# A hybrid decoder step: products with sides exchanged, queries never turned, decode memory attention by quarters of the array, and start-up loads moved between queues

## The chip, the cores and the metric

The kernel runs on one core of a Trainium2 chip. The time is the device time of that core in microseconds, the median of the runs shown. All arithmetic is in 32-bit floats. TensorE takes every 32-bit matmul as two instructions, so the trace shows two records for each matmul of the source; a transposition is one record.

## The reference, cut to what matters

One layer works on 1024 prompt tokens and 32 decode tokens (8 sequences of 4).

```
P = RMSNorm(x) @ w_in              # one projection, cut into the parts of three groups
A: mLSTM    4 heads x 256, in chunks of tokens, with a state matrix C and vector n per head
B: sparse   4 heads x 128, rotary; an indexer picks 256 keys per query; softmax; * silu(z)
C: memory   s = q . mem_k ; a = softmax(s) ; o = a . mem_v ; * silu(z)   (4 heads x 128, 256 memory rows)
y = x + RMSNorm(concat(A, B, C) @ w_out)
```

In group C the prompt attends to one set of memory keys, and each decode sequence b to its own (`cache_mem_k[b]`, `cache_mem_v[b]`, 256 x 512 each).

In group A, per head and chunk of 128 tokens, with decays:

```
s   = (q k^T) * decay ;   num = s v + inter * (q C)
C   = decay * C + (w k)^T v
```

## The kernel before, in words

Four stages run one after another: `project_rotate`, `select`, `attend_bc` and `mix_out`. Between two stages all engines meet (the wait is recorded at line 113) and the semaphores are cleared. Inside a stage each engine has its own list of instructions, written out in order, and waits on semaphores; DMAs are issued from SP's list, a few from ACT's and POOL's. Nothing reorders a list.

**project_rotate.** x is normalised, turned and kept as `xT` (model dimension on the partitions, tokens along the free axis). Most columns of w_in are multiplied in "tiles" (128 tokens by one block of columns, line 1065). Six blocks of 512 columns (`QUADS`) are multiplied by the seven-product scheme (`quad`, line 1129): the 2 x 2 blocks of x and w are summed by DVE, seven products of 512 tokens x 1024 x 256 columns are made, and ACT and DVE combine them out of PSUM. A product is four groups t = 0..3 of 128 tokens; each has 8 matmuls in which x is the stationary side and 256 columns of w move. Group t writes `bank[t][:, 0:256]`. Results are stored as rows of the scratch tensor `proj` (token by column). The decode tokens are done beside them by `quad_decode`.

Three of the six blocks are the memory queries (`C_MQ`) and the mLSTM queries (`C_Q`, `C_Q + 512`). While the later tiles are multiplied, rows of `proj` come back (`load_r`, line 713): queries and keys of group B, index queries and the memory queries. DVE and POOL rotate those of group B (`rotary`, lines 795 to 801); then PE turns five groups g per tile of 128 tokens (`turn_group`, line 1032; g = 0 is the memory queries), ACT copies each out of `rbank` (`keep_group`, line 942) and stores them in `headT`, the scratch tensor of turned heads. `hooks` says after which matmul of which tile each group is turned. The rotation of tile n + 1 waits until the stores of tile n have landed.

**select** picks the keys; it also projects the columns that are left. Near its end `ahead` loads the prompt memory keys, the decode memory keys of sequences 0 and 1, and the decode memory values of sequences 0 to 4 into the half of `w` that is free.

**attend_bc** first finishes what concerns the decode tokens, then walks through 32 units (8 tiles of 128 tokens x 4 heads) plus a lag of 6 slots, after which its share of w_out is multiplied (line 1933). The part for the decode tokens comes in this order on PE: turn the prompt memory keys (1836); wait for `lk_ready`, that is for DVE, which waits for twelve small DMAs (`small_in`); turn the selected logits (1842) and probabilities (1850); then for each of the 32 pairs of a sequence and a head turn its memory keys (two transpositions, 1869), ACT copies them (2040), DVE clears a 128 x 128 slot `pz` and puts the four queries in their columns (2152, 2153), and one matmul of 128 rows x 256 memory rows adds into `bank[4]` (1882); softmax over all rows at once (2159 to 2165); then 16 matmuls with a cleared slot each against 512 columns of memory values (1895), of which every row is kept for its own head only (`own_head`). SP loads the other six key tiles in a loop as their buffers come free (1767). DVE's `dec_clear` lets the 32 units begin.

**mix_out** does the mLSTM of group A and the rest of w_out. It walks through slots s = -2 .. 36: unit s + 2 is turned (`turn`, 2820: two transpositions for q, two for k), unit s + 1 gets its products of q and k (2831), unit s its numerator (2843, 2845) and its new state (2856); from s = 5 on (LAG) the output of an earlier chunk is multiplied by w_out (2882) in the same slot, and from s = 1 on one decode sequence and head per slot is done (2894, 2902). Unit n = 4 c + h is chunk c and head h. SP loads a unit with six DMAs (`load`, 2353 to 2355), unit s + 4 at the end of slot s. At its start SP issues, in this order: the gate rows, unit 0, seven tables (2366 to 2374), unit 1, `dv`, eight decode states (2379), units 2 and 3, two blocks of w_out of 2 MB (2385), the first rows of the partial output (2359), `g_post` (2387), and in slot 0 another 25 small DMAs (2394 to 2402), then the second partial rows.

## Time and profile before

| | |
|---|---|
| median of 3 runs | 3103.03 us (3101.26 to 3108.2) |
| the profiled execution, its own time | 3105.0 us |
| its span, first to last instruction | 3103.3 us |
| PE busy | 2944.9 us, 95% |
| DVE, ACT, POOL busy | 1399.9, 451.0, 404.1 us |
| mean granted clock of TensorE | 0.973 of full speed |
| project_rotate | 0 to about 1098 us |
| select | about 1098 to 2182 us |
| attend_bc | about 2182 to 2648 us |
| mix_out | about 2648 to 3103 us |

The page gives busy times of each engine over the span. A matmul's record includes its way through the array, so the time that a matmul costs in a long row of them is the distance between two starts: the length of a group less one record, divided by the number of records less one. A granted clock of 1.00 is 2.4 GHz, and 0.50 is 1.2 GHz. An idle time in square brackets stands ahead of the instruction, with what ended it.

### The profile page before, as it was taken

How to read it: one execution, taken by the hardware profiler on the slowest of the kernel's cores; microseconds unless marked ns; L12 is line 12 of the kernel's file. 1: busy time of each engine (PE TensorE's matmuls, PEld its weight loads, DVE VectorE, ACT ScalarE, POOL GpSimd, SP SyncE). 2: the span in 40 equal slices, each digit the busy share in tenths (PEclk: the TensorE clock that was granted, in tenths of full speed). 3: DMA queues.
4: the chain of work that ended last, by engine and by line, in shares of the span. 5: the costliest groups of instructions: out<-in, count | busy, mean ns of one | idle time of the engine just before them, and what ended most of it. 6: DMA issues, size and time to landing. Idle time of an engine off the chain costs nothing. (4 is left out here: it accounts for less than half of the span.)

```text
span 3103.3 us, 36094 instructions
## 1 busy us (share of the span) xinstructions
PE 2944.9 (95%) x13209; PEld 1757.9 (57%) x13209; DVE 1399.9 (45%) x2480; ACT 451.0 (15%) x970; POOL 404.1 (13%) x567
## 2 busy tenths in 40 slices
PE   8999999999999979999999999999689999499998
PEld 6678888888644434444444444444455564355553
DVE  3241111111121226899999998554332231244553
ACT  3210000000011135100000300000232221122221
POOL 0000000000022200000000000264013100233432
PEclk9999999999999988999999999999899999699999
DMA  6512112221526351320210521376464212745642
GB/s 235 119 33 77 61 46 68 75 70 50 170 83 199 113 194 27 116 73 20 75 72 20 182 73 55 108 240 197 139 207 150 90 49 85 245 128 182 193 148 90
DMA packets 248895, 353.59 MB, mean 114 GB/s; under 512 B 42412, under 2 KB 164756, under 8 KB 243484
## 3 DMA queue, kind: packets, MB, share of 16 engines
q1 hardware_dynamic: 207436, 269.86, 26.9%
q0 software_dynamic: 14784, 61.88, 6.4%
q10 hardware_dynamic: 26544, 20.08, 2.2%
q8 instruction: 87, 1.43, 0.2%
q14 instruction: 44, 0.36, 0.0%
HBM read 267.86 MB, written 86.43 MB: 114 GB/s over the span
## 5 line engine op out<-in xcount | busy, mean ns | idle before, releaser
L276 PE MATMUL sbank<-w,xT 128*128 128x512 f32 x2048 | 882.6, 593 | 6.6 <-ACTq L227 2.9
L276 PEld LDWEIGHTS sbank<-w,xT 128*128 128x128 f32 x2048 | 389.1, 190 | 496.2 <-issue 489.3
L1065 PE MATMUL bank<-w,xT 128*128 128x512 f32 (+1 forms) x768 | 290.9, 534 | 0.0
L1129 PE MATMUL bank<-w,xT 128*128 128x256 f32 x1152 | 253.9, 380 | 0.0
L1129 PEld LDWEIGHTS bank<-w,xT 128*128 128x128 f32 x1152 | 217.8, 190 | 30.3
L1933 PE MATMUL at_bank_bc<-w,at_hT 128*128 128x512 f32 x512 | 230.0, 593 | 3.9 <-ACT at_bc_out L2091 3.9
L1129 PE MATMUL bank<-w,area 128*128 128x256 f32 x960 | 212.1, 379 | 0.0
L1065 PEld LDWEIGHTS bank<-w,xT 128*128 128x128 f32 x768 | 143.4, 191 | 121.3 <-issue 106.2
L897 DVE TENSOR_TENSOR pout<-pout,bank 128x256 f32<-128x256 f32 x120 | 50.5, 421 | 339.6 <-PE bank L1129 339.6
L1129 PEld LDWEIGHTS bank<-w,area 128*128 128x128 f32 x960 | 182.4, 190 | 24.8
L1579 DVE MATCH_REPLACE8 area<-m,area 128x384 f32<-128x384 f32 (+2 forms) x192 | 165.7, 876 | 0.0
L1576 DVE MAX8 m<-area 128x8 f32<-128x384 f32 (+2 forms) x192 | 155.5, 879 | 11.9 <-DVE area L1579 11.9
L1933 PEld LDWEIGHTS at_bank_bc<-w,at_hT 128*128 128x128 f32 x512 | 94.6, 190 | 103.0 <-issue 101.6
L250 ACT ACTIVATE pout_b<-sbank 128x512 f32<-128x512 f32 x64 | 37.9, 598 | 787.8 <-PE sbank L276 787.8
L795 POOL TENSOR_TENSOR area<-area 128x288 f32<-128x288 f32 (+1 forms) x9 | 11.7, 1299 | 907.3 <-DMA area<-in_rot 727.3
L853 DVE TENSOR_TENSOR w<-w 128x2048 f32<-128x2048 f32 x24 | 54.4, 2288 | 166.6 <-PE bank L1129 163.2
L1129 PE MATMUL bank<-w 128*128 128x256 f32 x576 | 129.2, 379 | 0.0
L1129 PEld LDWEIGHTS bank<-w 128*128 128x128 f32 x576 | 109.4, 190 | 14.9
L2882 PE MATMUL mo_bank_acc<-mo_w_out_a,mo_hT 128*128 128x512 f32 x256 | 116.2, 598 | 0.0
L2882 PE MATMUL mo_bank_acc<-area,mo_hT 128*128 128x512 f32 x256 | 116.2, 598 | 0.0
L795 DVE TENSOR_TENSOR area<-area 128x512 f32<-128x512 f32 (+1 forms) x9 | 6.2, 691 | 201.8 <-DMA headT<-area 184.9
L980 ACT ACTIVATE pout<-bank 128x256 f32<-128x256 f32 x48 | 18.4, 384 | 502.0 <-PE bank L1129 502.0
(384 smaller groups left out, 3324.7 us busy)
## 6 DMA issues: line engine op xcount, KB each, us to landing
w<-in_w_in SPq DMA_DIRECT2D x18, 2048.0 KB, 12.5
w<-in_w_in SPq DMA_DIRECT2D x28, 1024.0 KB, 5.3
area<-in_x_prompt SPq DMA_DIRECT2D x16, 1024.0 KB, 7.4
proj<-pout_b SPq DMA_DIRECT2D x64, 256.0 KB, 2.1
proj<-pout SPq DMA_DIRECT2D x96, 128.0 KB, 1.7
headT<-area ACTq DMA_DIRECT2D x8, 1024.0 KB, 9.2
area<-roped_q_of_decode POOLq DMA_DIRECT2D x32, 256.0 KB, 3.9
w<-in_w_out SPq DMA_DIRECT2D x4, 2048.0 KB, 15.9
```

Source lines behind the costliest of these rows:

```text
L250: copy(pout[:, j, 0:self.w], bank[:, 0:self.w], function).then_inc(self.copied, 1)
L276: last = k.nc.tensor.matmul(bank[0:r, 0:self.w], k.xT[:, c, r0:r0 + r], k.w[:, u, c, 0:self.w], start=c == 0, stop=c == KT - 1)
L795: order(ops.tensor_tensor(o1, x1, cos, ALU.mult))
L853: nc.vector.tensor_tensor(quarter[out], quarter[x], quarter[y], op).then_inc(w_sums, 1)
L897: nc.vector.tensor_tensor(out[:, t, :], x[:, t, :], bank[t][:, 0:256], ALU.add).then_inc(sums_read, 1)
L980: nc.scalar.activation(out[:, t, :], bank[t][:, 0:256], ACT.Copy).then_inc(first_read, 1)
L1065: last = nc.tensor.matmul(dst[:, 0:wd], k.xT[:, c, t * P:(t + 1) * P], wc, start=c == 0, stop=c == KT - 1)
L1129: last = nc.tensor.matmul(bank[t][:, 0:256], x(c, t), at[name][:, c, :], start=first and c == 0, stop=c == 7, skip_group_check=True)
L1576: order(nc.vector.max(m8[:, j, :], x))
L1579: order(nc.vector.match_replace(out=x, in_to_replace=m8[:, j, :], in_values=x, imm_value=TAKEN))
L1933: last = nc.tensor.matmul(acc[:, :], hT[:, t % 2, j, :], w[:, j, b * O_W:(b + 1) * O_W], start=j == 0, stop=j == HT - 1)
L2882: last = nc.tensor.matmul(acc[n % 2][:, :], hT[:, c % 2, j, :], w[b][:, j, :], start=j == 0, stop=j == HT - 1)
```

## The change

1. **Sides exchanged in three of the six seven-product blocks** (`TURNED`: memory queries and both halves of the mLSTM queries). In them the weights are the stationary side, 128 columns at a time, and 512 tokens move: two groups (t = 1 and t = 3) of 8 matmuls of 512 in place of four groups of 8 matmuls of 256. A group fills a whole bank, `bank[0]` or `bank[2]`, and counts as two; ACT and DVE read the same 128 x 256 pieces as before through `product_at`. The results come out turned, and are stored so: the memory queries into `headT`, the mLSTM queries into a new scratch tensor `qT`.
2. **No turning of queries later.** In `project_rotate` the memory queries of the eight prompt tiles are neither loaded, nor turned, copied or stored again (the decode tile still is). ACT's store of a tile into `headT` is two DMAs that leave the four memory-query slots out. In `mix_out` a unit's q is loaded turned (from `qT`, 256 rows of 128 tokens), `turn` has two transpositions in place of four, ACT's copy is 256 wide in place of 512, and `dots` and `scaled_q` read the loaded q.
3. **Decode memory attention by quarters.** `ahead` loads five key tiles and two value tiles; the other three and six are loaded at the start of `attend_bc`. All decode queries are spread once into `dmq_of`. Per sequence PE turns all four heads (8 transpositions into two banks), ACT and DVE copy one bank each, and four matmuls, each into its own 32 rows of `bank[4]`, add the dots. This comes before the work on the selected logits, whose instructions DVE does between the copies. The values are 64 matmuls of 32 rows x 128 columns out of a spread tile, each for its own head, so that `own_head` goes for this part.
4. **Loads at the start of `mix_out`.** SP issues only the gate rows and units 0 to 3. ACT issues the tables and `dv` (8 DMAs) ahead of its first copy, four decode states in slot -1 and four in slot 1. POOL issues the two blocks of w_out in slot 0 and `g_post` in slot 2. The partial rows come in slot 1 on SP, the 25 small DMAs in slot 10 (`LATE`), and DVE's two instructions that need them in slot 14.

The core of the diff:

```diff
+    TURNED = [C_MQ, C_Q, C_Q + 512]
...
+        def product_at(n, t):
+            return bank[t // 2 * 2][:, 256 * (t % 2):256 * (t % 2) + 256] if fp.QUADS[n] in fp.TURNED else bank[t][:, 0:256]
...
+        def group(n, g):
+            return 4 * n + g - 1 if n < QT else 4 * QT + g
+        def stored_all(n):
+            return 80 * n
...
             if q >= 2 and q % 2 == 0:
-                found.update({0: (q // 2 - 1, 4), 12: (q // 2, 0)})
+                found[0] = (q // 2 - 1, 4)
...
-            if q == 1:
-                found[1] = (0, 0)
+            if q == 2 * QT:
+                found[12] = (QT, 0)
...
-                act.dma_start(k.headT[:, 0:T_IK, at_], keep_at[:, 0:T_IK, 0:r]).then_inc(r_stored, 16)
+                if n < QT:
+                    for a, b in ((T_Q, T_MQ), (T_IQ, T_IK)):
+                        act.dma_start(k.headT[:, a:b, at_], keep_at[:, a:b, 0:r]).then_inc(r_stored, 16)
+                else:
+                    act.dma_start(k.headT[:, 0:T_IK, at_], keep_at[:, 0:T_IK, 0:r]).then_inc(r_stored, 16)
...
                         for c in range(8):
-                            last = nc.tensor.matmul(bank[t][:, 0:256], x(c, t), at[name][:, c, :],
-                                                    start=first and c == 0, stop=c == 7, skip_group_check=True)
-                        last.then_inc(product, 1)
+                            if whole:
+                                u = t // 2
+                                last = nc.tensor.matmul(bank[2 * u][:, :], at[name][:, c, P * u:P * (u + 1)], x(c, 0, SEQ // 2),
+                                                        start=first and c == 0, stop=c == 7, skip_group_check=True)
...
+                        last.then_inc(product, 2 if whole else 1)
...
+            def turn_mkd(b):
+                if b < 5:
+                    pe.wait_ge(mkd_in[b], 16)
+                else:
+                    pe.wait_ge(mkd_late[b - 5], 16)
+                if b >= 2:
+                    pe.wait_ge(mkd_kept_a, b - 1)
+                    pe.wait_ge(mkd_kept_v, b - 1)
+                for h in range(H):
+                    for c in range(2):
+                        last = nc.tensor.transpose(
+                            bank[(5, 2)[b % 2] + h // 2][:, N_MEM * (h % 2) + P * c:N_MEM * (h % 2) + P * (c + 1)],
+                            mkd[b % 5][:, c, h * DH:(h + 1) * DH], k.ident[:])
+                last.then_inc(mkd_turned, 1)
+            def dots_mkd(b):
+                pe.wait_ge(mkd_kept_a, b + 1)
+                pe.wait_ge(mkd_kept_v, b + 1)
+                for h in range(H):
+                    last = nc.tensor.matmul(bank[4][NS * h:NS * (h + 1), 0:N_MEM], dmq_of[:, h, NS * b:NS * (b + 1)],
+                                            mkdT[:, b % 2, h, :], start=b == 0, stop=b == DEC_B - 1)
+                last.then_inc(mdots, 1)
...
+            for b in range(DEC_B):
+                for c in range(2):
+                    for h in range(H):
+                        last = nc.tensor.matmul(bank[6][NS * h:NS * (h + 1), 0:DH], spread[:, c, h, NS * b:NS * (b + 1)],
+                                                mvd[:, 2 * b + c, h * DH:(h + 1) * DH], start=b + c == 0,
+                                                stop=b == DEC_B - 1 and c == 1)
...
+    LATE = 10
...
-                for dst, c0 in ((q, C_Q), (kk, C_K), (o, C_O), (z, C_Z)):
+                sp.dma_start(q[:, r, :, :], k.qT[h * ML_D:(h + 1) * ML_D, at].rearrange("(c p) t -> p c t", p=P)
+                             ).then_inc(loaded[r], 16)
+                for dst, c0 in ((kk, C_K), (o, C_O), (z, C_Z)):
...
+            def load_states(b):
+                for h in range(ML_H):
+                    act.dma_start(ds[:, ML_H * b + h, :, 0:ML_D], ins["state_mlstm_C"][b, h].rearrange("(c p) v -> p c v", p=P)
+                                  ).then_inc(d_state_in[ML_H * b + h], 16)
...
+                if s == 0:
+                    for b in range(2, O_B):
+                        nc.gpsimd.dma_start(w[b], ins["w_out"][0:ML_W, b * O_W:(b + 1) * O_W]
+                                            .rearrange("(c p) n -> p c n", p=P)).then_inc(w_in[b], 16)
+                if s == 2:
+                    nc.gpsimd.dma_start(g[:], ins["g_post"][0:1, :].partition_broadcast(P)).then_inc(g_in, 16)
...
-                for x, at in ((q, 0), (kk, 2)):
-                    for c in range(2):
-                        last = nc.tensor.transpose(tq[:, (at + c) * P:(at + c + 1) * P],
-                                                   x[:, n % 4, c * P:(c + 1) * P], k.ident[:])
+                for c in range(2):
+                    last = nc.tensor.transpose(tq[:, c * P:(c + 1) * P], kk[:, n % 4, c * P:(c + 1) * P], k.ident[:])
```

## Rows read from the trace of the kernel before

**Rows 1.** Windows: length, then busy us of PE, PEld, DVE, ACT, POOL, clock, DMA, GB/s.
```profile
2150.00:2250.00 100.00, 73.96 (x368) 43.84 (x366) 26.46 (x121) 17.33 (x43) 7.57 (x8) 0.86 0.46 153
...
2660.00:2710.00 50.00, 22.45 (x111) 16.53 (x112) 12.47 (x45) 6.79 (x19) 15.32 (x28) 0.64 0.97 309
...
2680.00:2685.00 5.00, 4.63 (x34) 3.32 (x35) 1.89 (x6) 0.50 (x2) 1.65 (x3) 1.00 1.05 394
...
2720.00:2730.00 10.00, 7.93 (x25) 5.76 (x25) 5.06 (x20) 1.94 (x5) 3.14 (x6) 0.67 0.51 132
...
2900.00:3000.00 100.00, 100.00 (x378) 58.41 (x377) 48.50 (x139) 20.95 (x58) 36.16 (x59) 1.00 0.54 169
```
**Rows 2.** Waits of PE: waiter, releaser, us in total, times, longest.
```profile
PE mo_bank_turn_qk L2820 <- DMA mo_rows_everywhere<-gate_rows: 31.5, 4, 16.8
```
**Rows 3.** Timeline of PE, projection: start, us, line, tiles, count, [idle before].
```profile
111.82 20.77 PE L1057 MATMUL bank<-w,memT 128*128 128x512 f32 x48
...
259.61 13.98 PE L1129 MATMUL bank<-w,xT 128*128 128x256 f32 x64
```
**Rows 4.** Timeline of PE while heads are turned in the projection.
```profile
826.67 1.11 PE L1032 MATMUL rbank<-ident_sb,area 128*128 128x128 f32 x4 [2.84 <-DMA area<-in_rot]
...
833.64 0.60 PE L1032 MATMUL rbank<-ident_sb,area 128*128 128x128 f32 x4
834.08 2.74 PE L1065 MATMUL bank<-w,xT 128*128 128x512 f32 x6
...
956.06 0.66 PE L1032 MATMUL rbank<-ident_sb,area 128*128 128x128 f32 x4 [1.87 <-DVEq L904]
```
**Rows 5.** The page, part 6: a DMA, count, KB each, us to landing.
```profile
headT<-area ACTq DMA_DIRECT2D x8, 1024.0 KB, 9.2
```
**Rows 6.** Timeline of PE from the last projection to the first unit of attend_bc.
```profile
2171.35 3.70 PE L273 MATMUL sbank<-w,xT 128*32 128x128 f32 x128
2181.66 1.94 PE L1836 MATMUL at_bank_dots<-ident_sb,w 128*128 128x128 f32 x8 [6.61 <-PEq L113]
2193.95 0.69 PE L1842 MATMUL at_bank_mem<-ident_sb,at_lk 128*128 128x128 f32 x2 [10.35 <-DVEq L2133]
...
2235.12 14.00 PE L1895 MATMUL at_bank_bc<-w,at_pz 128*128 128x512 f32 x32
...
2251.75 0.49 PE L1919 MATMUL at_bank_dots<-area,at_qT 128*128 128x128 f32 x2 [1.77 <-DVEq L2184]
```
**Rows 7.** Timeline of DVE and DMA issues, start of attend_bc.
```profile
2182.35 1.98 DVE L2116 MEMSET at_p_spread<- 128x2304 f32 x1 [0.43 <-issue]
...
at_dec_mqT<-headT SPq DMA_DIRECT2D x1, 64.0 KB, 3.2
```
**Rows 8.** Timeline of PE, start of mix_out.
```profile
2653.71 0.69 PE L2820 MATMUL mo_bank_turn_qk<-ident_sb,mo_q 128*128 128x128 f32 x2 [3.03 <-DMA mo_rows_everywhere<-gate_rows]
...
2678.02 0.44 PE L2820 MATMUL mo_bank_turn_qk<-ident_sb,mo_q 128*128 128x128 f32 x2
...
2702.54 0.69 PE L2820 MATMUL mo_bank_turn_qk<-ident_sb,mo_q 128*128 128x128 f32 x2 [16.84 <-DMA mo_rows_everywhere<-gate_rows]
...
2710.74 0.38 PE L2820 MATMUL mo_bank_turn_qk<-ident_sb,mo_q 128*128 128x128 f32 x2
...
2731.45 3.60 PE L2882 MATMUL mo_bank_acc<-area,mo_hT 128*128 128x512 f32 x8
```
**Rows 9.** Timeline of SP's DMA issues, start of mix_out.
```profile
2650.41 0.57 SPq L2355 DMA_DIRECT2D mo_rows_everywhere<-gate_rows  x1
...
2694.35 0.43 SPq L2355 DMA_DIRECT2D mo_rows_everywhere<-gate_rows  x1
```
**Rows 10.** Timeline of PE, one steady slot of mix_out.
```profile
2766.20 0.38 PE L2820 MATMUL mo_bank_turn_qk<-ident_sb,mo_q 128*128 128x128 f32 x2
2766.42 0.38 PE L2820 MATMUL mo_bank_turn_qk<-ident_sb,mo_k 128*128 128x128 f32 x2
...
2777.59 0.38 PE L2820 MATMUL mo_bank_turn_qk<-ident_sb,mo_q 128*128 128x128 f32 x2
```

More of the change, by code:

```diff
@@ L1019, in turn_group @@
                 if g == 0:
-                    pe.wait_ge(r_loaded[u], 80 * (n // 2 + 1))
-                    heads = [mq[0:r, u, h * DH:(h + 1) * DH] for h in range(H)]
+                    pe.wait_ge(mq_in, 16)
+                    heads = [mq[0:r, h * DH:(h + 1) * DH] for h in range(H)]
                 elif g < 3:
@@ L1090, in quad @@
                         (of(rows_d), "22", False))):
-                    for t in range(4):
+                    whole = fp.QUADS[n] in fp.TURNED
+                    for t in (1, 3) if whole else range(4):
+                        opening = t == 1 if whole else t == 0
                         if phase == 0:
-                            if t == 0:
+                            if opening:
                                 loaded("11")
@@ L1128, in quad @@
                         for c in range(8):
-                            last = nc.tensor.matmul(bank[t][:, 0:256], x(c, t), at[name][:, c, :],
-                                                    start=first and c == 0, stop=c == 7, skip_group_check=True)
-                        last.then_inc(product, 1)
+                            if whole:
+                                u = t // 2
+                                last = nc.tensor.matmul(bank[2 * u][:, :], at[name][:, c, P * u:P * (u + 1)], x(c, 0, SEQ // 2),
+                                                        start=first and c == 0, stop=c == 7, skip_group_check=True)
+                            else:
+                                last = nc.tensor.matmul(bank[t][:, 0:256], x(c, t * P, (t + 1) * P), at[name][:, c, :],
+                                                        start=first and c == 0, stop=c == 7, skip_group_check=True)
+                        last.then_inc(product, 2 if whole else 1)
             at = None
@@ L2113, in _, with keep_mkd @@
             order = Order(dve, order_sem)
-            for ap, value in ((ones, 1.0), (zero, 0.0)):
-                order(nc.vector.memset(ap[:], value))
+            nc.vector.memset(dmq_of[:], 0.0).then_inc(dmq_set, 1)
+            order(nc.vector.memset(ones[:], 1.0))
+            dve.wait_ge(dmq_in, 16)
+            dve.wait_ge(dmq_set, 1)
+            nc.vector.tensor_copy(dmq_of[:, :, :].rearrange("p h (b x) -> p h b x", x=36)[:, :, :, 0:DEC_T],
+                                  dmq[:, :, :].rearrange("p h (b t) -> p h b t", t=DEC_T)).then_inc(dmq_set, 1)
+            def keep_mkd(b):
+                dve.wait_ge(mkd_turned, b + 1)
+                if b >= 2:
+                    dve.wait_ge(mdots, b - 1)
+                nc.vector.tensor_copy(mkdT[:, b % 2, 2:4, :].rearrange("p a b -> p (a b)"), bank[(5, 2)[b % 2] + 1][:, :]
+                                      ).then_inc(mkd_kept_v, 1)
+            for b in range(4):
+                keep_mkd(b)
             nc.vector.memset(spread[:], 0.0).then_inc(masks, 1)
-            dve.wait_ge(small_in, 16 * (4 + 2 * DEC_T))
+            keep_mkd(4)
+            keep_mkd(5)
+            dve.wait_ge(small_in, 16 * (3 + DEC_T))
             for c in range(2):
```

323 lines of the change are left out of this document (153 added, 170 removed).

## The prediction, written before the change was run

> **What bounds the kernel now.** I read the windows by stretch first. In a steady stretch late in the kernel PE is busy all the time at full clock: there only work taken off PE counts [rows 1]. Two stretches are different. Where attend_bc begins, PE is idle 26 us of 100, and where mix_out begins, it is busy only 22.45 us of 50, with DMA at 97% [rows 1]. Next the waits of PE: the longest sum is 31.5 us in four waits, all for a unit of mix_out that had not been loaded [rows 2]. Then the timeline of PE, for the order within these two starts [rows 6, 8], and that of the projection, for what a transposition or a product costs [rows 3, 4]. So the terms to look for are PE work removed where PE is full, and idle time removed at the two starts.
>
> **Part 1, the exchanged products.** A record of 256 moving columns costs (13.98 - 0.379) / 63 = 0.2159 us, taking the 0.379 us of one record off; one of 512 columns costs (20.77 - 0.597) / 47 = 0.4292 us [rows 3]. A block of seven products has 7 x 4 x 8 x 2 = 448 records now, 96.7 us, and 224 after, 96.1 us: 0.6 us each, 1.8 us for three. The reads of ACT and DVE keep their number and size. A group now lasts 16 x 0.43 = 6.9 us and the next one that writes the same bank begins 6.9 us after it ends, while its two reads take under 1 us, so no wait is added. Bounds: 0 (if the new form costs what two of the old do) and 3 us. I take 1.8.
>
> **Part 2a, the memory queries no longer turned in the projection.** Four transpositions hold PE from 833.64 to 834.08, 0.44 us [rows 4]. Eight tiles make 3.5 us. For tile 0 they save nothing: the rotation that the next group needs starts when `load_r` has landed (the wait that ended at 826.67 [rows 4]) and takes some 7 us, so the 2.84 us wait moves from the first group to the second. It ends earlier only by the 256 KB less that come before, 0.8 us. So 0.8 + 7 x 0.44 = 3.9 us. The single wait of 1.87 us at 956.06, for the rotation of tile 4 [rows 4], hangs on the store of `headT`, 1 MB in 9.2 us [rows 5]. A quarter of those bytes goes, some 2 us, so I take this wait as gone too: 5.8 us in all. The extra DMA issue per tile is on ACT, mostly idle here. Bounds: 2 us (store no faster, tile 0 nothing, half of the transpositions hidden) and 7.
>
> **Part 3, decode memory attention.** Before, from 2181.66 to 2251.75, 70.1 us [rows 6]. It holds a 10.35 us wait for small DMAs and 14.00 us of value matmuls [rows 6]. After:
> - 2181.66 to 2183.4: prompt memory keys turned, as before. The clock is at 1.2 GHz here: 8 transpositions cost (1.94 - 0.42) / 7 = 0.217 us each [rows 6]. The first sequence is turned until 2185.1.
> - The decode queries are now SP's first DMA of the stage. It took 3.2 us to land [rows 7], so it is there at 2184.9. Clearing `dmq_of` (1152 columns) is half of the 1.98 us that 2304 took [rows 7], and is done by then. PE goes on at 2185.3.
> - Eight sequences. At half clock one costs 8 x 0.217 = 1.74 us of transpositions, and 8 records of dots. Four matmuls into four quarters ran side by side in the projection: 128 records of 128 columns in 3.70 us, 0.029 us each at full clock [rows 6]; at 256 columns and half clock that is 0.11, so 0.9 us. Together 2.6 us, at full clock 1.3. The copies (0.6 us on ACT, 0.7 on DVE, my estimate from other 128x512 reads) fit beside. DVE's extra 2 us memset and the logits add about 2 us at full clock. Half of the sequences at each clock: 4 x 2.6 + 3 x 1.4 + 2 = 17 us, to 2202; all at half clock, to 2206.
> - The tail: softmax of the memory rows, two turnings, softmax of the selected rows, then 128 records at 0.029, 3.7 us, one copy. With some ten short steps of 0.2 to 0.7 us between: 10.5 us at full clock, 14 at half.
> The first unit then starts between 2212 and 2220, instead of 2251.75: 32 to 39 us, and I take 35. What could hold it is data: before the values can be used, three key tiles, six value tiles (4.5 MB) and 2 MB of gathered values must land in the 24 us from 2182. That needs 270 GB/s, and DMA has moved 394 in a busy stretch [rows 1]. Outer bounds 22 and 43. The six value tiles, the prompt values and units 0 and 1 are queued behind SP's waits for key buffers, but those end by 2190. The w_out loads keep their distance to the values' end.
>
> **Part 4, the start of mix_out.** Now: the first unit is turned at 2653.71, the fourth at 2678.02 (slot 1), the fifth only at 2702.54 after 16.84 us idle, and the first w_out product starts at 2731.45 in slot 5 [rows 8]. The fifth unit's last DMA was issued at 2694.35, 44 us after the first unit's [rows 9], since 25 small DMAs and 8 MB of others stood ahead in SP's list.
> - After, units 0 to 3 are issued one behind the other, 3 us each. The constants come 3 to 4 us sooner, from ACT. POOL's and DVE's work of slots -1 and 0 is unchanged and becomes the chain. I put slot 1 at 2670, 8 us sooner (bounds 4 and 12).
> - Unit 4 is issued when slot 0 ends and should land within slot 1, so the 16.84 us go. Slots 1 to 4 each take what slots 3 and 4 take now: (2731.45 - 2710.74) / 2 = 10.3 us at a mean granted clock of 0.67 [rows 1, 8], or about 7.7 at full clock, as slot 1 did. With 9.5: slot 5 at 2670 + 38 = 2708, 23 us sooner. Bounds: all at 10.3 with slot 1 at 2674, 2715; all at 7.7 from 2666, 2697: 16 to 34 us. A late unit takes more off (rival 1).
> - POOL issues 4 MB with two instructions; I take 1 us each, behind its wait for DMAs.
>
> **Part 2b, steady slots of mix_out.** PE is full there, and the two q transpositions hold it from 2766.20 to 2766.42, 0.22 us of an 11.39 us slot [rows 10]. Slots 5 to 29: 25 x 0.22 = 5.5 us. The new q load moves the same bytes in pieces half as long. The 25 small DMAs in slot 10 take SP some 12 us, one slot. Unit 14 is then issued about 5 us late, with some 5 us to spare: I charge 0.5 us (0 to 3). Net 5.0.
>
> **Sum.** 1.8 + 5.8 + 35 + 23 + 5.0 = 70.6 us. The profiled execution took 3105.0 us (span 3103.3), 2 us more than the median 3103.03; its differences carry over to the median: 3032 us. Its own range, with the bounds not all on one side, is 3017 to 3046.
>
> **Rival 1: bytes, not issue order, hold mix_out's start.** Before unit 5 can be turned (slot 3, 2687 by my working), the queues hold units 0 to 5 (4.7 MB), tables 0.9, states 2.1, w_out 4.2, partial rows 2.1, x 1.05 and g 1: 16 MB. At the 309 GB/s of the stretch 2660 to 2710 [rows 1] this takes 52 us from 2648, to 2700: 13 us late. For it: DMA is already at 97% there, and SP issues 3 MB of partial rows and x ahead of unit 5. Against it: 394 GB/s was reached at 2680 [rows 1], by which it is 2689, and w_out, on another queue, need not be through. Part 4 then gives 10 instead of 23: 3045 us. The Trainium skill ("DMA: Bandwidth & Descriptors", section "Issuing engines are not separate DMA queues") states that DMAs issued by SP, ACT and POOL interleave on the same 16 engines, so that issuing from several saves only the sequencer's time. By that rule alone moving w_out to POOL buys no room, which is this rival; the DMA share of 97% in rows 1 agrees with it.
>
> **Rival 2: the decode part stays a chain.** If TensorE stays at half clock and the late tiles or DVE's list hold each sequence to 4 us (32 us for eight, and a 14 us tail), the first unit starts at 2232: part 3 gives 20 instead of 35, 3047 us. For it: after the present idle time the clock stayed at 0.50 for long. Against it: PE has far fewer gaps.
>
> **Rival 3: slower.** The half-long pieces of q make a unit's loads land late in every steady slot. Unit s + 4 is issued in 2.7 us at the end of slot s and is wanted one slot, 11.2 us, later: it decides when landing takes over 8.5 us, and PE then loses what is over. At 11.5 us it loses 3 us in each of 27 slots, 81 us against the 76 that the rest gives: 3108 us. For it: stores in such pieces took 9.2 us, but for 1 MB [rows 5]; a unit's q is 128 KB. Against it: the steady DMA share is 0.54 [rows 1].
>
> That the change does not do what it says: if the turned blocks cost two reads' wait per group, 42 groups x 0.8 us = 34 us come back, 3066 us. The waits are a whole group away, so I give it little.
>
> **Chances.** Forecast 0.58, rival 1 0.23, rival 2 0.12, rival 3 0.02, the last 0.03, else 0.02. Faster or slower by 0.2% is 6 us, about what a measurement of this kernel can tell: faster 0.95, same 0.02, slower 0.03. The range takes in the rivals 1 and 2 and the bounds of parts 3 and 4: 3013 to 3055.
>
> **What would show it.** Right: records of 128x512 in the three blocks at 0.429 us apart; no wait at L1032's first group but one on the rotation; the first unit of attend_bc some 31 to 39 us after the stage's first transposition instead of 70; turns of unit 4 without a long wait, and 43 to 61 us, some 54, from the first turn of mix_out to its first w_out product, instead of 78; steady slots of 11.2 us. Wrong: PE waiting on DMAs for units 4 to 6, or on the value tiles; a slot at s = 12 with a wait; reads in the blocks that PE waits for.

## The result and the profile after

The changed kernel takes 3055.57 us (median of 4 runs, 3044.59 to 3060.49) against 3105.61 for the kernel before in the same comparison (3101.26 to 3109.45): ratio 0.9838, interval 0.9821 to 0.9854, 50 us less. The forecast was 3032 us, 70.6 us less than the 3103.03 known then: the time is 24 us above it and half a microsecond above the end of its range, 3055, and 20 us of the gain are missing. Three executions far from all others (6806.11 us in experiment 1, 3534.25 and 12586.81 us of the kernel before, taken beside experiments 9 to 12) are left out of every median and ratio here. The profiled execution is the slowest of the four, 3060.49 us with a span of 3058.8; its gain is 44.5 us. The four executions are 3060.49, 3059.81, 3051.32 and 3044.59 us, twice as far apart as those of before; that turns out to be part of the answer.

The first part of the page: PE has 28.5 us less to do, in 12529 matmuls, and its share of the span is 95% as before.

```profile
PE 2916.4 (95%) x12529; PEld 1607.7 (53%) x12529; DVE 1387.1 (45%) x2392; ACT 429.8 (14%) x937; POOL 405.2 (13%) x570
```

The waits of PE in the changed kernel (in all, times, longest). Before, the first line had 31.5 us with one wait of 16.8 [rows 2]; the line with L276 was not there at all.

```profile
PE mo_bank_turn_qk L2886 <- DMA mo_rows_everywhere<-gate_rows: 17.3, 4, 7.3
...
PE sbank L276 <- issue: 10.2, 2, 5.6
...
PE rbank L1062 <- DVEq L930: 4.4, 1, 4.4
PE mo_bank_dots_num L2908 <- DVE mo_sd L2513: 4.3, 1, 4.3
PE at_bank_turn L1906 <- DVE w L2169: 4.3, 3, 2.4
```

**Projection.** The timeline of PE where the seven-product blocks end and the tiles begin (start, duration, line, count, and in brackets the idle time before and what ended it):

```profile
794.43 10.03 PE L1164 MATMUL bank<-w 128*128 128x512 f32 x23
804.30 19.90 PE L1095 MATMUL bank<-w,xT 128*128 128x512 f32 x46
828.60 1.12 PE L1062 MATMUL rbank<-ident_sb,area 128*128 128x128 f32 x4 [4.40 <-DVEq L930]
829.51 3.93 PE L1095 MATMUL bank<-w,xT 128*128 128x512 f32 x6
...
1089.37 2.89 PE L1401 MATMUL sbank<-ident_sb,w 128*128 128x128 f32 x12 [9.97 <-PEq L113]
```

The 23 records of the exchanged products take (804.30 - 794.43) / 23 = 0.429 us each, as forecast. The first group turned is now a rotated one and waits 4.40 us for DVE, where 2.84 and 1.87 us were idle before [rows 4]. Select's first transposition starts at 1089.4 instead of 1098.3.

**Select**, which the change doesn't touch, gives all of that back and more: attend_bc's first transposition starts at 2187.50, 5.8 us *later* than before [rows 6]. The windows (length, busy time of PE, PEld, DVE, ACT and POOL, granted clock, DMA share, GB/s) and the timeline of PE at the two idle stretches:

```profile
1700.00:1710.00 10.00, 9.02 (x141) 5.52 (x139) 9.68 (x18) 0.88 (x2) 0.00 (x0) 1.00 0.07 26
1710.00:1720.00 10.00, 5.34 (x7) 2.37 (x8) 9.47 (x19) 2.54 (x3) 0.00 (x0) 0.66 0.75 219
```

```profile
1714.66 20.60 PE L276 MATMUL sbank<-w,xT 128*128 128x512 f32 x42 [5.64 <-issue]
...
1949.42 8.96 PE L276 MATMUL sbank<-w,xT 128*128 128x512 f32 x14 [4.60 <-issue]
```

PE idles 5.64 and 4.60 us waiting for nothing that a semaphore shows ("issue"). Both stand where TensorE jumps back to the head of its loop over the select stage's column blocks (line 282). The loop has four iterations of some 230 us, each of two blocks of 114, and so three jumps back: the first, near 1480 us, passes without idle time, the second and the third don't. Behind it the clock falls to its lower level, 1.2 GHz: 0.66 on the mean of 1710 to 1720. The stage's block products take 936.7 us instead of 922.0, 7.3 us for each of the two, of which 5.1 are idle. The DMA view of the same stretch says what moved. Changed kernel, 1600 to 2100 us:

```profile
DMA packets 27368, 59.26 MB, mean 119 GB/s; under 512 B 3111, under 2 KB 3623, under 8 KB 27352
## 3 DMA queue, kind: packets, MB, share of 16 engines
q8 instruction: 16, 0.26, 0.2%
```

Sixteen packets of 16 KB of instructions; the same view of the kernel before has no row for q8. There the last packet of instructions comes at 1487 us, in the first iteration, and the next at 2209, behind the stage: three jumps back with nothing read. Its loop runs from what it has at hand, and the changed kernel's is read again.

**Decode memory attention**, timeline of PE: first transposition, a wait for copies, the value products, the first attend unit.

```profile
2187.50 1.94 PE L1881 MATMUL at_bank_dots<-ident_sb,w 128*128 128x128 f32 x8 [6.63 <-PEq L113]
...
2197.49 1.08 PE L1906 MATMUL at_bank_turn<-w,at_dec_mqT_spread 128*32 128x256 f32 x8 [2.39 <-DVE w L2169]
...
2215.46 6.43 PE L1941 MATMUL at_bank_bc<-w,at_p_spread 128*32 128x128 f32 x128 [2.28 <-DMA w<-in_cache_mem_v]
...
2222.45 0.49 PE L1966 MATMUL at_bank_dots<-area,at_qT 128*128 128x128 f32 x2 [0.55 <-DVEq L2226]
```

From the first transposition to the first unit it is 34.95 us instead of 70.1 [rows 6].

**Start of mix_out**, timeline of PE: the stage's first product, the turning of units 0, 3, 4, 5 and 6, and the first product with w_out (slot 5).

```profile
2620.80 1.05 PE L2975 MATMUL mo_bank_acc<-ident_sb,mo_y 12*128 12x12 f32 x9 [9.03 <-DMA mo_y<-gate_rows]
2629.13 0.69 PE L2886 MATMUL mo_bank_turn_qk<-ident_sb,mo_k 128*128 128x128 f32 x2 [7.28 <-DMA mo_rows_everywhere<-gate_rows]
...
2645.53 0.44 PE L2886 MATMUL mo_bank_turn_qk<-ident_sb,mo_k 128*128 128x128 f32 x2
...
2660.66 0.44 PE L2886 MATMUL mo_bank_turn_qk<-ident_sb,mo_k 128*128 128x128 f32 x2 [4.57 <-DMA mo_rows_everywhere<-gate_rows]
...
2671.50 0.56 PE L2886 MATMUL mo_bank_turn_qk<-ident_sb,mo_k 128*128 128x128 f32 x2 [3.03 <-DMA mo_rows_everywhere<-gate_rows]
...
2679.12 0.38 PE L2886 MATMUL mo_bank_turn_qk<-ident_sb,mo_k 128*128 128x128 f32 x2
...
2689.51 1.02 PE L2947 MATMUL mo_bank_acc<-area,mo_hT 128*128 128x512 f32 x2
```

From first turn to first w_out product 60.4 us instead of 77.7 [rows 8]. But the first turn itself is 8.3 us behind the stage's first product; it was 4.1. From 2645 to 2671 us, where units 4 and 5 are late, the DMA engines are busy throughout (share 1.04, 387 GB/s).

**Steady slots**, timeline of PE, and the first and the last of the 25 small transfers of slot 10 on SyncE's queue. The slots are 11.17 us apart (before 11.39 [rows 10]); behind slot 10 unit 14 is late once.

```profile
2701.48 0.38 PE L2886 MATMUL mo_bank_turn_qk<-ident_sb,mo_k 128*128 128x128 f32 x2
2712.65 0.38 PE L2886 MATMUL mo_bank_turn_qk<-ident_sb,mo_k 128*128 128x128 f32 x2
...
2772.14 0.44 PE L2886 MATMUL mo_bank_turn_qk<-ident_sb,mo_k 128*128 128x128 f32 x2 [2.44 <-DMA mo_rows_everywhere<-gate_rows]
```

```profile
2750.84 0.47 SPq L2431 DMA_DIRECT2D mo_dec_o<-proj  x1
...
2762.35 0.43 SPq L2439 DMA_DIRECT2D mo_dec_y<-y_of_groups_b_c_decode  x1
```

### The profile page after: what moved, and what is told of

Read it like the earlier page. It is cut to its first block and busy times, and to the rows that moved or that the text cites. A ratio compares the mean times of both kernels' runs of the same rounds, so it can differ in the third digit from the quotient of the medians.

```text
span 3058.8 us, 34334 instructions
## 1 busy us (share of the span) xinstructions
PE 2916.4 (95%) x12529; PEld 1607.7 (53%) x12529; DVE 1387.1 (45%) x2392; ACT 429.8 (14%) x937; POOL 405.2 (13%) x570
## 5 line engine op out<-in xcount | busy, mean ns | idle before, releaser
L276 PE MATMUL sbank<-w,xT 128*128 128x512 f32 x2048 | 887.7, 596 | 15.7 <-issue 10.2
L276 PEld LDWEIGHTS sbank<-w,xT 128*128 128x128 f32 x2048 | 391.0, 191 | 508.5 <-issue 503.6
L1095 PEld LDWEIGHTS bank<-w,xT 128*128 128x128 f32 x768 | 144.1, 191 | 125.8 <-issue 110.8
L1167 PE MATMUL bank<-w,xT 128*128 128x256 f32 x576 | 127.2, 380 | 0.0
L1164 PE MATMUL bank<-xT,w 128*128 128x512 f32 x288 | 126.4, 595 | 0.2 <-issue 0.2
L1167 PEld LDWEIGHTS bank<-w,xT 128*128 128x128 f32 x576 | 108.8, 190 | 15.9 <-issue 0.8
L1167 PE MATMUL bank<-w,area 128*128 128x256 f32 x480 | 106.0, 379 | 0.0
L1164 PE MATMUL bank<-area,w 128*128 128x512 f32 x240 | 104.5, 592 | 0.0
L1167 PEld LDWEIGHTS bank<-w,area 128*128 128x128 f32 x480 | 91.2, 190 | 12.4
```

The costliest lines, as they stand in the source:

```text
L276: last = k.nc.tensor.matmul(bank[0:r, 0:self.w], k.xT[:, c, r0:r0 + r], k.w[:, u, c, 0:self.w], start=c == 0, stop=c == KT - 1)
L1095: last = nc.tensor.matmul(dst[:, 0:wd], k.xT[:, c, t * P:(t + 1) * P], wc, start=c == 0, stop=c == KT - 1)
L1164: last = nc.tensor.matmul(bank[2 * u][:, :], at[name][:, c, P * u:P * (u + 1)], x(c, 0, SEQ // 2), start=first and c == 0, stop=c == 7, sk ...
L1167: last = nc.tensor.matmul(bank[t][:, 0:256], x(c, t * P, (t + 1) * P), at[name][:, c, :], start=first and c == 0, stop=c == 7, skip_group_ ...
```

## The experiments

This table is read off the timelines of PE in the profiled execution of each kernel: us from the first product of the blocks to the first tile (blocks), to select's first transposition (tiles), to the first 128x512 product of its column blocks (indexer), to attend_bc's first transposition (columns), to its first unit (decode), to mix_out's first product (units), to its first turn (unit 0), to its first w_out product (slots 0-4), to the end (rest). The times are good to 0.1 us, and each row is one execution; the last column is the median of its executions (experiment 8 has one).

| kernel | blocks | tiles | indexer | columns | decode | units | unit 0 | slots 0-4 | rest | median, us |
|---|---|---|---|---|---|---|---|---|---|---|
| before | 610.6 | 289.2 | 161.4 | 922.0 | 70.1 | 397.9 | 4.1 | 77.7 | 371.9 | 3105.6 |
| changed | 606.5 | 285.1 | 161.4 | 936.7 | 34.9 | 398.4 | 8.3 | 60.4 | 369.3 | 3055.6 |
| 1 decode alone | 609.5 | 288.6 | 161.4 | 922.1 | 31.6 | 396.2 | 4.0 | 77.9 | 372.0 | 3067.1 |
| 2 turned alone | 607.0 | 290.9 | 161.4 | 930.1 | 69.1 | 399.4 | 3.7 | 80.3 | 367.2 | 3105.5 |
| 3 order alone | 609.8 | 287.5 | 161.7 | 922.1 | 69.0 | 396.2 | 8.2 | 60.1 | 373.8 | 3092.5 |
| 4 changed again | 606.9 | 287.6 | 161.5 | 923.5 | 31.9 | 398.6 | 7.6 | 59.9 | 369.3 | 3049.0 |
| 5 loop written out | 607.0 | 284.8 | 161.3 | 921.4 | 31.2 | 400.5 | 7.8 | 59.9 | 370.6 | 3045.6 |
| 6 y later | 606.8 | 287.6 | 161.4 | 930.1 | 32.0 | 396.9 | 8.9 | 60.4 | 369.3 | 3056.1 |
| 7 w_out later | 607.1 | 286.8 | 161.1 | 938.2 | 32.0 | 395.1 | 8.1 | 66.3 | 369.0 | 3057.9 |
| 8 small spread | 606.8 | 286.5 | 161.1 | 931.0 | 32.8 | 396.7 | 9.2 | 59.0 | 366.8 | 3049.3 |
| 9 turned, written out | 606.0 | 284.7 | 159.5 | 920.5 | 71.3 | 397.9 | 3.6 | 82.2 | 366.7 | 3091.7 |
| 10 before, written out | 611.2 | 288.0 | 161.5 | 920.5 | 69.4 | 397.2 | 4.0 | 73.9 | 371.9 | 3098.8 |
| 11 gain later | 608.0 | 287.6 | 161.7 | 929.7 | 32.2 | 397.7 | 6.2 | 58.8 | 369.3 | 3046.8 |
| 12 combined | 606.6 | 286.3 | 160.9 | 921.9 | 31.8 | 395.1 | 6.2 | 58.2 | 366.7 | 3038.2 |
| 13 changed, shifted | 607.2 | 307.0 | 156.2 | 922.6 | 31.6 | 396.8 | 8.3 | 60.6 | 370.5 | 3063.2 |
| 14 before, shifted | 611.0 | 305.5 | 154.8 | 930.0 | 70.8 | 399.1 | 4.0 | 72.2 | 371.9 | 3118.5 |
| 15 groups later | 607.0 | 278.7 | 161.3 | 922.0 | 33.2 | 395.3 | 6.1 | 58.2 | 366.8 | 3031.9 |

The first four ran together (before: 3103.14), then 5 to 8 (3103.66), 9 to 12 (3098.79) and 13 to 15 (3103.27).

**1 to 3: the parts one by one.** Each takes the lines of one part into the kernel before and nothing else.

```
1  + for b in range(DEC_B): turn_mkd(b + 1); dots_mkd(b)       # and all of the decode part
2  + TURNED = [C_MQ, C_Q, C_Q + 512]                           # and all that reads turned queries
3  + LATE = 10; tables on ScalarE, w_out on GpSimd, units 0 to 3 first
```

> The kernel before with the new decode memory attention alone (projection, select and mix_out as before). Theory (the parts add up): the first attend unit comes 35 us after the stage's first transposition instead of 70, and all of it reaches the end: 3105 - 35 = 3070 us. Rival (the gain of this part in the full change came partly from the shorter projection, or is given back at mix_out's start because the same bytes come later): 3080 or more. If the select stage's idle products (5 us before a group of 128x512 products, seen in the changed kernel near 1714 and 1949 us) are a matter of the execution and not of the turned blocks, they can show here too and add some 8 us each.

> The kernel before with the turned blocks alone (memory and mLSTM queries multiplied with the sides exchanged, mix_out reading the queries turned; loads in the old order, decode part as before). Theory: select begins 9 us sooner, a steady slot of mix_out is 0.2 us shorter (5 us in all), the slots at mix_out's start lose two transpositions each (0 to 3 us): 3105 - 15 = 3090 us if the select stage keeps its length. Rival (the turned blocks themselves cost the select stage 15 us, by where its loop then lies in the instruction stream): no gain, 3100 to 3106, with the idle products of the changed kernel in the profile.

> The kernel before with mix_out's new load order alone. Theory (bytes hold units 4 and 5, order only unit 4): slot 5 comes 10 to 13 us sooner against the stage's first product than the 82 us of before, one wait of 2.4 us appears at slot 12 behind the 25 small transfers: 3105 - 10 = 3095 us. Rival (my forecast: the order alone was the bound): 23 us sooner, 3082 us.

Decode alone: 3067.06 us (3062.76 to 3074.84), ratio 0.9901 (0.9872 to 0.9930). Decode takes 31.6 us instead of 70, and no later stretch of the profile gives any of it back. The executions are too few to say more: 31 us by the ratio, with 22 to 40 in its interval, for the 38.5 of the profile. Turned alone: 3105.52, ratio 1.0009 (0.9995 to 1.0023): nothing. Its steady part is 4.7 us shorter and its blocks 3.6, but the column blocks are 8.1 longer, with one idle product of the kind that the rival named, and slots 0-4 are 2.6 longer:

```profile
PE sbank L276 <- issue: 4.4, 1, 4.4
```

Order alone: 3092.48, ratio 0.9967 (0.9958 to 0.9977): unit 0 and slots 0-4 together 68.3 us instead of 81.8, 13.5 less, and 1.9 more in the rest. As expected, not as forecast (23).

**4 and 5: is it the execution or the loop?** The changed kernel unedited, and with the loop written out:

```
-        with pe.Fori(first, self.n // 2) as i:
+        for i in range(first, self.n // 2):
```

> The changed kernel once more, unedited. Theory (the two idle stretches of 5 us in the select stage, each with 7 us of half clock behind it, come and go between executions): some executions near 3044, others near 3060, and the profile of this one can show the select stage 8 or 16 us shorter. Rival (they belong to this program and come every time): all near 3058, select as long as in the first profile.

> The changed kernel with TensorE's loop over the select stage's column blocks written out (no jump back), everything else as it is. Theory (where the jump back finds the head of the loop no longer at hand, TensorE waits for its instructions: 4.4 to 5.6 us, then 7 us at half clock, once or twice in an execution): no idle before the 128x512 products of this stage but the small ones, the stage from its first block product to the next stage's first transposition at 922 us in every profile, executions closer together and near the low end of the changed kernel's, 3044 to 3049 us. Rival (the idle comes from the transfers of that moment, the queries of the gates being turned by ScalarE): the idle of some 5 us near 1710 us stays, and the times spread as before, 3044 to 3060.

Unedited: 3048.43, 3049.59, 3060.19, 3044.19 us. Its profiled execution, 3048.43, has no idle product: the waits of PE from 1260 to 2170 us are these two lines, and no instructions were read between 1600 and 2100.

```profile
PE sbank L276 <- ACT pout_b L255: 2.4, 3, 0.8
PE sbank L276 <- PE sbank L273: 1.3, 4, 0.3
```

So the same program does both. Written out: 3043.83 to 3047.15, ratio 0.9817 (0.9801 to 0.9833), columns 921.4. The interval overlaps that of the changed kernel, so the proof is in the stretch and not in the total. Instructions are read all the time now (the DMA view from 1600 to 2100 us), and PE never waits for them; straight code is read ahead.

```profile
DMA packets 27620, 59.79 MB, mean 120 GB/s; under 512 B 3137, under 2 KB 3649, under 8 KB 27608
## 3 DMA queue, kind: packets, MB, share of 16 engines
q8 instruction: 12, 0.20, 0.2%
```

The rival (transfers of that moment) is out: they are the same in both. One profile alone would not show it, since the fourth has no idle product either. But the turned blocks with the loop written out were profiled four times (5, 9, 12 and 15) and never had one; with the loop they had one or two in six of seven profiles (changed, 2, 6, 7, 8 and 11, but not 4).

**6 and 7: the bytes ahead of units 4 and 5.**

```
6  - if s == 1: load_part(0) ... load_part(1)       + if s == 2: the same
   - if s == 1: ... sp.dma_start(xin[:, :], ...)    + if s == 3: the same
7  - if s == 0:  (GpSimd) for b in range(2, O_B): nc.gpsimd.dma_start(w[b], ...)
   + if s == 3:  the same
```

> The changed kernel with the two y parts loaded in slot 2 and the x block in slot 3 of mix_out instead of slot 1 (3 MB behind unit 5's loads instead of ahead of them). Theory (bytes: the 3 MB stand ahead of unit 5's six transfers): TensorE's wait for unit 5 (2.7 to 3.0 us) goes, SyncE issues unit 5's six transfers in 3 us instead of 10, slot 5 comes 2 to 5 us sooner against the first turn, 3 us less in all; unit 4's wait stays, since it is issued before them. Rival (rotation of the slots by the decode step and DVE holds them): slot 5 no sooner than 59.9 us behind the first turn.

> The changed kernel with the two late w_out blocks (4 MB) issued on GpSimd in slot 3 of mix_out instead of slot 0. Theory (bytes: the 4 MB move while unit 4's and 5's loads want to land): TensorE's waits for unit 4 (4.6 to 5.7 us) and unit 5 shrink to under 2 us together, slot 5 4 to 6 us sooner against the first turn. Rival (unit 4 is issued too late, when the first slot ends, so its 5 us landing shows whatever else moves): unit 4's wait stays above 3 us. A third: the w_out blocks now come too late, with a new wait before slot 7's products.

With y and x later unit 5's wait is gone and slot 5 is no sooner: 60.4 us. The timeline of PE shows what holds the slots when no transfer does:

```profile
2664.11 0.38 PE L2886 MATMUL mo_bank_turn_qk<-ident_sb,mo_k 128*128 128x128 f32 x2
...
2667.00 1.20 PE L2896 MATMUL mo_bank_dots_num<-mo_qT,mo_kT 128*128 128x128 f32 x4 [2.51 <-DVE mo_a L2533]
...
2674.31 0.38 PE L2886 MATMUL mo_bank_turn_qk<-ident_sb,mo_k 128*128 128x128 f32 x2
...
2677.16 1.20 PE L2896 MATMUL mo_bank_dots_num<-mo_qT,mo_kT 128*128 128x128 f32 x4 [2.47 <-DVE mo_a L2533]
...
2684.51 0.38 PE L2886 MATMUL mo_bank_turn_qk<-ident_sb,mo_k 128*128 128x128 f32 x2
```

Two slots of 10.20 us, no transfer waited for, at a granted clock of 0.66: PE makes the numerator, DVE the denominator, ACT the square, POOL the root, DVE the output, and the next unit's products wait for it. Unit 4 was still 4.85 us late in this run. With w_out in slot 3, unit 4 is in time (no wait), but the 4 MB now stand in the way of unit 5:

```profile
2674.72 0.69 PE L2886 MATMUL mo_bank_turn_qk<-ident_sb,mo_k 128*128 128x128 f32 x2 [13.39 <-DMA mo_rows_everywhere<-gate_rows]
```

Slots 0-4 take 66.3 us. So bytes do make units 4 and 5 late: either wait goes when the transfers ahead of it are moved. How much they cost together is not shown, since no run has all units in time. An estimate from the two clean slots is 4 x 10.2 = 41 us for slots 1 to 4, against 44.0 in the changed kernel; against it stands slot 1 of experiment 7, which took only 6.2 us with unit 4 in time.

**8: the 25 small transfers.**

```
-                if s == LATE:
-                    for h in range(ML_H):
+                if LATE <= s < LATE + ML_H:
+                    for h in (s - LATE,):
```

> The changed kernel with the 25 small transfers of mix_out's slot 10 issued six in each of slots 10 to 13 and one in slot 14. Theory (SyncE spends 12 us on them and issues unit 14's loads that much later): TensorE's wait of 2.4 us at slot 12 goes and slot 5 to the end takes 366.9 us instead of 369.3. Rival (the wait comes from the bytes of the moment): it stays.

The wait is gone and the rest takes 366.8 us, 2.5 less (experiment 12, with the same edit, has 366.7): they cost 2.4 us, not the 0.5 that I charged.

**9 and 10: the loop written out where only the queries are turned, and in the kernel before.**

> The turned blocks alone (as in the second experiment, which timed 3105.5 us, no gain over 3103.1) with TensorE's loop over the select stage's column blocks written out. Theory (the turned blocks are worth some 7 us, and the jump back in the select loop took them away): select's block products in 922 us instead of 930, 3096 to 3098 us, 0.998 of before with all of its interval under 1. Rival (the turned blocks are worth nothing by themselves): 3103 us or more.

> The kernel before with the same loop written out. Theory (its loop already runs without the idle, 922 us in the profiles of the kernel before and of both variants without turned blocks): 3100 to 3104 us, within 0.1% of before. Rival (each kernel loses by its jumps, so that writing the loop out is worth the same 5 us anywhere): 3098 us or less.

Turned alone goes from 1.0009 to 0.9969 (0.9956 to 0.9981), 3091.68 us; the kernel before stays at 0.9999 (0.9989 to 1.0010). The turned blocks are worth 7 us by the medians and 10 by the ratio (6 to 14), and the jump had taken them away; the kernel before pays nothing for its own jump.

**11 and 12: ScalarE's large tables behind unit 0, and the three edits together.**

```
+            act.wait_ge(loaded[0], 96)
             act.dma_start(gain[:, :], ...)    # 512 KB, now with a semaphore of its own
             act.dma_start(dv[:, :, 0:ML_D], ...)
```

> The changed kernel with ScalarE's transfers of the head gain (512 KB) and of the decode values (128 KB) held back until unit 0 of mix_out has landed. Theory (ScalarE's transfers share the engines with unit 0's, which lands 3.5 to 4.3 us later than in the old order): the first turn of mix_out 4 to 5 us behind the stage's first product instead of 7.6 to 9.2, slot 5 some 3 us sooner against that product (65 us instead of 68). Rival (what holds unit 0 is units 1 to 3, issued right behind it on SyncE): the first turn stays at 7.5 us or more. A third: the products of slot 0 wait for the gates instead, as the gain is late, and slot 5 does not move.

> The changed kernel with the select loop written out, the 25 small transfers spread over slots 10 to 14, and the head gain and decode values held back behind unit 0. Theory (the three add up): 5 us from the loop (median of the changed kernel 3050 to 3056, written out 3045.6), 2.4 from slot 12, 3 from mix_out's start: 3040 us. Rival (only the loop counts): 3045 us.

Unit 0 comes 6.2 us behind the first product instead of 7.6 to 9.2, and slot 5 at 65.0 instead of 67.5 to 68.9: some 3 us. Unit 0 lies between theory (4 to 5) and rival (7.5 or more), so ScalarE's transfers are one part of what the new order cost there. The rest, some 2 us to the 4.1 of before, was not isolated; units 1 to 3 behind it on SyncE are the candidate. The total, 3036.7 to 3052.4 us, is not to be told from the changed kernel's. The Trainium skill ("DMA: Bandwidth & Descriptors", section "Issuing engines are not separate DMA queues") states that transfers issued by different engines run on the same 16 DMA engines and interleave; this trace agrees, with unit 0 sooner by 1.5 to 3 us once ScalarE's 640 KB were held back. Combined: 3038.2 us, ratio 0.9804 (0.9785 to 0.9823).

**13 and 14: why this loop and not that one.** In the built programs the loop's body is 1560 instructions, 98 KB, in both kernels. It begins at instruction 12480 in the changed kernel and 13896 before; a packet of 16 KB brings 256 instructions (written out, an iteration reads six packets), so it begins at place 192 of a packet, or 72. The traces bear the two places out: the next packet is read 22 us behind the loop's first product in the kernel before and in experiments 1 and 3, and 1 to 2 us behind it in the changed kernel and in 2, 4, 6, 7, 8 and 11. Shifted, experiment 13 has 22 us and 14 has 1. The edit puts idle increments ahead of it: 136 in the changed kernel (place 72), 120 in the kernel before (place 192).

```
+            for _ in range(136):        # 120 in the kernel before
+                pe.sem_inc(shifted, 1)
```

> The changed kernel with 136 semaphore increments on TensorE at the head of the select stage, so that the loop begins at the same place within a block of 256 instructions as before (72 instead of 192). Theory (place): no idle of 4 to 6 us before the block products, that stretch 922 us in the profile, executions at 3044 to 3050, median some 5 us under the changed kernel's 3050 to 3056. Rival (the turned blocks themselves, or the length of the stream ahead): idle in the profile, executions up to 3060.

> The kernel before with 120 semaphore increments at the same point, so that its select loop begins at place 192 of a block, as in the changed kernel. Theory (place): the idle appears, once or twice in most executions, the stretch of block products 930 us or more instead of 922, median 3105 to 3110 us against 3100 to 3103 of before. Rival: 922 us and no difference.

The increments are not free (0.155 us each: the wait at the head of select grows from 10 to 31.1 and 28.7 us, and 5 to 7 us of it come back in the indexer), so the medians can't be read directly; the columns can. The changed kernel at place 72: 922.6 us, no idle product, no instructions read from 1600 to 2100, four executions within 2.2 us (3062.81 to 3064.96), where the changed kernel's eight lie 16 us apart. The kernel before at place 192: 930.0 us, and for the first time in a kernel without turned blocks:

```profile
PE sbank L276 <- issue: 4.5, 1, 4.5
PE sbank L276 <- ACTq L227: 2.9, 1, 2.9
```

Place decides whether the idle can come, in both directions: at place 192 seven of eight profiles have it (all but 4), at place 72 none of four (before, 1, 3 and 13), and both shifted kernels carry increments, so the increments are not the cause. The Trainium skill ("Runtime: NRT & Kernel Launch", section "Instruction fetch mechanics") states that TensorE's instruction memory holds 128 KB, is filled strictly in order in blocks of 256 instructions, and that a taken branch to a target outside the current window of two blocks has to fetch first and stalls. The window of two blocks does not agree with this case: in the kernel before, three jumps back over 1560 instructions read nothing (no packet from 1487 to 2209 us). The 128 KB do agree: they are eight blocks, and the body lies over seven. That the place changes how much is read past the loop's end (place 96 of its last block or 216) is my reading, and no run shows it. Nor is it shown why the same program misses in some executions only.

**15: the turning of the rotated columns later**, on top of the combined kernel.

```
-                at = (7, 10, 13) if n == 0 else (6, 9, 12) if n < QT else (3, 6, 9, 12)
+                at = (13, 14, 15) if n == 0 else (6, 9, 12) if n < QT else (3, 6, 9, 12)
```

> The combined kernel of the twelfth experiment (3038.2 us) with the turning of the first tile's three groups of rotated columns after products 13, 14 and 15 of its tile instead of 7, 10 and 13. Theory (TensorE waits 4.3 us there for the rotation): the wait falls to about 2 us and 3 to 7 us of half clock behind it shrink, 2 to 4 us less: 3035 us. Rival (the turning releases the next tile's rotation, which then is as much later and is waited for at 953 us): no change, the wait moves there.

3031.92 us, ratio 0.9774 (0.9759 to 0.9789): the best of all, 6 us under the combined kernel by the medians and 9 by the ratios, whose intervals just overlap. The tiles take 278.7 us instead of 286.3, more than expected: no wait is left from 800 to 1085 us, and the granted clock, 0.93 in the mean around the wait of 4.16 us, stays at 1.00. The window from 800 to 850 us in the combined kernel and in this one:

```profile
800.00:850.00 50.00, 45.84 (x111) 20.65 (x110) 8.14 (x10) 3.14 (x6) 7.20 (x6) 0.93 0.51 169
```

```profile
800.00:850.00 50.00, 50.00 (x128) 22.69 (x127) 9.42 (x12) 3.14 (x6) 8.43 (x7) 1.00 0.58 191
```

## Why the prediction was right in direction and 24 us too low

- **Not in it at all: select.** The sum has five terms and none for this stage: I took a stage that the change doesn't touch as unchanged. Its column blocks take 14.7 us more in the profiled execution, 16 in one other (7), 8 to 9 in four (2, 6, 8, 11) and 1.5 in one (4). This is the largest error of the profiled execution. By the ratios it is 12 us where only the queries are turned (1.0009 against 0.9969 written out); in the changed kernel it is 3 to 10 by the medians (3049.0 and 3055.6 against 3045.6) and 6.5 by the ratios, less than what part 4 lacked. Without it (3045.6) the prediction would have missed by 14 us, inside the range that ended at 3055. The number of misses differs between executions of one program, so the median of four moves with it: the same kernel's second four have 3049.0, inside the range too.
- **Part 4, 23 us: 13.** Order alone gives 13.5 less 1.9 in the rest. The step that failed first is "I put slot 1 at 2670, 8 us sooner": unit 0 landed 4.2 us later behind ScalarE's and SyncE's other transfers, so slot 1 was 3.7 us sooner, counted from the stage's first product. Then "slots 1 to 4 each take ... 9.5": they took 44.0 us, not 38. Unit 4 did not land within slot 1 (4.57 us) and unit 5 was 3.03 late, but in the two slots of experiment 6 that wait for no transfer the chain from PE over DVE, ACT and POOL takes 10.2 us at this clock too. By that estimate timely units would have saved some 3 of the 6 us. The bound of 10.3 that I had worked out was the value to take, since no clock gain followed (granted 0.62 from 2671 to 2689 us, 0.67 before). Rival 1 was nearer with its total (10), and half right: its bytes do make units 4 and 5 late, but moving its 3 MB away brought slot 5 no sooner, and moving its 4 MB of w_out made it later.
- **Part 2a, 5.8 us: 4.1 in the profile, about 1.5 over all.** Ten kernels with turned blocks take 284.7 to 290.9 us for the tiles (mean 286.8), four without 287.5 to 289.2. The step "the 1.87 us wait is gone" held in the first profile and failed in others: 2.35, 1.12, 1.23 and 1.11 us stand there in experiments 2, 4, 6 and 11. Nor is it the mark of the old kernel: 1, 3, 10 and 14, whose stores are the old ones, have no such wait near 956 us, so that its absence in one profile says nothing of the stores. And I counted the first group's wait as 2.84 us moved; it became 4.40. What holds this part is DVE's rotation; experiment 15 shows it was worth 7.6 us.
- **Part 2b, 5.0 us: 2.6.** The slot went from 11.39 to 11.17 as forecast, and turned alone gains 4.7 in the rest. The 0.5 us charged for the 25 small transfers was the step that failed; it was 2.44.
- **Part 1, 1.8 us: 3 to 4.** The products cost what I computed; the kernels with turned blocks take 606.0 to 608.0 us, those without 609.5 to 611.2. What gives the other 1 to 2 us I haven't isolated.
- **Part 3, 35 us: 35.1** in the profile and 38 elsewhere (31.2 to 33.2 us against 69.0 to 71.3). Right: the turning and dots of the eight sequences end 21.0 us behind the stage's first transposition (forecast 20 to 24), and the tail took some 14, the forecast for half clock. Within the tail two misses are hidden: the value products took 6.43 us at a granted clock of 0.56, not 3.7, and waited 2.28 for a tile. Rival 2, a chain that stays, is out.
- Of the signs that I had named for being wrong, three came: PE waiting on transfers for units 4 and 5, on a value tile, and in the slot at s = 12.
- Sum of the profiled execution: 4.1 + 4.1 - 14.7 + 35.1 - 0.5 + 13.1 + 2.6 = 43.8, with 0.7 from the start before the blocks, 44.5.

## What to carry to other kernels

Look for long loops on the engine that bounds the kernel. Here an edit that took 1416 instructions out ahead of a loop of 1560 moved it to another place in its packet, and each jump back that then missed cost 7 to 8 us, in a stage nobody touched. Other body sizes were not tried. Write such a loop out, and compare the stretch, not the total. Where a wait goes, ask what the chain behind it takes at the clock that the idle time leaves; and a stall of a few us on a full TensorE costs more than its length: the 4.2 us of experiment 15 were worth 7.6.

## What the runs showed of the hardware that I had not expected

- A loop of 1560 TensorE instructions made three jumps back with no instruction read (before, 1487 to 2209 us). Moved by its place in a packet, it was read again with idle of 4.3 to 5.6 us at one or two of the three jumps, or at none, the same program in different executions (3044 to 3060 us).
- A semaphore increment that nothing waits for cost TensorE 0.155 us ((31.1 - 10.0) / 136, and (28.7 - 10.2) / 120 in the other kernel).
- Eight executions of the changed kernel spread by 0.5%, four with the loop written out by 0.1% (3043.8 to 3047.2). The spread alone proves nothing: ten executions of experiment 9, written out too, spread by 0.3%.
